# Attention in a two-layer hybrid backbone: the multiplication of the probabilities moves from VectorE to GpSimd

## The reference

```python
def softmax_with_sink(s, sink):                       # group A: 8 heads of 64, 2 KV heads
    m = jnp.maximum(jnp.max(s, axis=-1, keepdims=True), sink)
    e = jnp.exp(s - m)
    return e / (jnp.sum(e, axis=-1, keepdims=True) + jnp.exp(sink - m))

def mla_core(qn, qr, kn, kr, v):                      # group C: 4 heads, 96 wide
    s = (jnp.einsum('bqhd,bkhd->bhqk', qn, kn)
         + jnp.einsum('bqhd,bkd->bhqk', qr, kr)).astype(jnp.float32) * MLA_SCALE
    p = jax.nn.softmax(s, axis=-1).astype(v.dtype)
    o = jnp.einsum('bhqk,bkhd->bqhd', p, v)
```

## Time and profile before

| what | value |
|---|---|
| median of 3 runs | 1774.49 us (1768.44 to 1776.2) |
| the profiled execution, first to last instruction | 1772.8 us |
| TensorE busy | 1656.5 us, 93% |
| VectorE busy | 448.1 us, 25% |
| ScalarE busy | 309.7 us, 17% |
| GpSimd busy | 43.0 us, 2% |

### The profile page before, as it was taken

The page is one execution under the profiler, slowest core; times in us unless marked ns, Lnnn a source line. Parts: engine busy times, 40 slices in busy tenths (PEclk is TensorE's granted clock), DMA queues, the critical chain, the costliest instruction groups (busy, mean ns, idle before and its releaser), DMA issues.

```text
span 1772.8 us, 21037 instructions
## 1 busy us (share of the span) xinstructions
PE 1656.5 (93%) x7998; PEld 937.7 (53%) x7999; DVE 448.1 (25%) x1098; ACT 309.7 (17%) x721; POOL 43.0 (2%) x49
## 2 busy tenths in 40 slices
PE   3999879999999999999998999899989989999988
PEld 1454445444444444445665765685536555865464
DVE  1367794210000000003588330100201101001011
ACT  3135453210000000002345221000101010000110
POOL 1001000100000000000010100000000000000000
PEclk9999999999999999999999989999999999999999
DMA  9530610252141122115304269987799999977997
GB/s 379 223 143 0 246 41 25 89 223 91 71 166 71 71 73 93 71 71 231 125 11 180 73 255 422 390 291 278 292 420 421 422 422 422 377 269 290 422 421 324
DMA packets 56605, 394.76 MB, mean 223 GB/s; under 512 B 6480, under 2 KB 7888, under 8 KB 8912
## 3 DMA queue, kind: packets, MB, share of 16 engines
q1 hardware_dynamic: 56384, 393.63, 56.1%
q10 hardware_dynamic: 144, 0.01, 0.0%
HBM read 392.57 MB, written 1.05 MB: 222 GB/s over the span
## 4 chain that ended last, share of the span: by engine, by line
PE 79%; DMA 10%; DVE 7%; issue 2%; ACT 1%; SPq 1%; DVEq 0%; ACTq 0%
PE ps L688 17%; DMA ring<-in_stream 10%; PE ps L764 10%; PE ps L470 9%; PE ps L773 9%; PE ps L708 9%; PE ps L668 5%; PE ps L812 4%; PE ps L809 3%; PE ps L416 2%; PE ps L867 1%; PE ps L592 1%; PE ps L745 1%; PE ps L796 1%; DVE arena L1358 1%
## 5 line engine op out<-in xcount | busy, mean ns | idle before, releaser
L688 PE MATMUL ps<-hT,ring 128*128 128x512 f32 x704 | 302.7, 592 | 0.0
L764 PE MATMUL ps<-ring,arena 128*64 128x256 f32 x1056 | 243.2, 384 | 20.9 <-DMA ring<-in_stream 14.3
L767 PE MATMUL ps<-ring,arena 128*64 128x256 f32 x1056 | 243.7, 384 | 0.0
L688 PEld LDWEIGHTS ps<-hT,ring 128*128 128x128 f32 x704 | 133.5, 190 | 167.3 <-issue 166.4
L764 PEld LDWEIGHTS ps<-ring,arena 128*64 128x64 f32 x1056 | 139.9, 137 | 92.7 <-issue 33.6
L470 PE MATMUL ps<-hT,ring 128*128 128x512 f32 (+2 forms) x480 | 172.5, 515 | 2.4 <-ACT hT L921 2.2
L773 PE MATMUL ps<-ring,arena 128*128 128x256 f32 x704 | 155.6, 379 | 0.0
L708 PE MATMUL ps<-arena,ring 128*128 128x512 f32 x352 | 151.2, 592 | 0.0
L773 PEld LDWEIGHTS ps<-ring,arena 128*128 128x128 f32 x704 | 132.2, 190 | 17.1
L767 PEld LDWEIGHTS ps<-ring,arena 128*64 128x64 f32 x1056 | 140.0, 137 | 0.0
L470 PEld LDWEIGHTS ps<-hT,ring 128*128 128x128 f32 (+1 forms) x480 | 87.9, 185 | 81.7 <-issue 73.7
(11 more groups left out here) (188 smaller groups left out, 1345.7 us busy)
## 6 DMA issues: line engine op xcount, KB each, us to landing
ring<-in_stream SPq DMA_DIRECT2D x371, 1024.0 KB, 13.1
xT<-in_x SPq DMA_DIRECT2D x8, 256.0 KB, 4.2
cst<-in_consts SPq DMA_DIRECT2D x1, 1092.0 KB, 23.8
out_x<-xT SPq DMA_DIRECT2D x4, 256.0 KB, 2.6
par<-in_params SPq DMA_DIRECT2D x2, 75.0 KB, 2.3
cst<-in_consts SPq DMA_DIRECT2D x1, 128.5 KB, 2.2
moep<-in_moe SPq DMA_DIRECT2D x1, 36.0 KB, 25.5
ccol<-in_c ACTq DMA_DIRECT2D x1, 8.0 KB, 2.4
```

The source lines that it names most:

```text
L688: last = pe.matmul(ps[:, 2 * m + f % 2, :], ring[:, slot, m * 1024 + k * P:m * 1024 + (k + 1) * P], hT[:, k, :], start=(k == 0), stop=(k = ...
L764: a = pe.matmul(ps[0:64, b, 0:256], hTe[:, k, 0:64], ring[:, s1, k * 256:(k + 1) * 256], start=(k == 0), stop=(k == KD - 1))
L767: last = pe.matmul(ps[64:P, b, 0:256], hTe[:, k, 0:64], ring[:, s3, k * 256:(k + 1) * 256], start=(k == 0), stop=(k == KD - 1))
```

## The change

The two multiplications of `shares` go from VectorE's list to GpSimd's. VectorE ends with the reciprocal and raises a new semaphore, `share_ready`; GpSimd waits for it, multiplies both heads and raises `soft_done`. `rden` gets a second buffer. GpSimd's instruction is `tensor_scalar` with two multiplications (by `rden`, then by 1.0), where VectorE's had one.

```diff
-        rden = sb("rden", [P, 2])
+        rden = sb("rden", [P, 2, 2])
...
+        share_ready = sem("share_ready")
...
+            def shares(layer, a):
+
+                stream_ = attention_units(layer)[a][2]
+                n = att_at[layer, a]
+                b = n % 2
+                gps.wait_ge(share_ready, n)
+                for hh in range(2):
+                    v = probs[:, 2 * b + hh, 0:T - stream_ * NX]
+                    last = gps.tensor_scalar(v, v, rden[:, b, hh:hh + 1], 1.0, ALU.mult, ALU.mult)
+                last.then_inc(soft_done, 1)
+
...
                 last.then_inc(spread_done, 1)
+                for a in range(len(attention_units(layer))):
+                    shares(layer, a)
                 for norm in (1, 2) if layer == 0 else (3,):
                     add_squares(norm)
...
-                chained(dve.reciprocal(rden[:, :], total))
-                for hh in range(2):
-                    v = probs[:, 2 * b + hh, 0:w]
-                    last = dve.tensor_scalar(v, v, rden[:, hh:hh + 1], None, ALU.mult)
-                last.then_inc(soft_done, 1)
+                dve.reciprocal(rden[:, b, :], total).then_inc(share_ready, 1)
```

More of the change, by code:

```diff
@@ L1344, in shares @@
             def shares(layer, a):
-                kind, _, stream_, _ = attention_units(layer)[a]
+                kind = attention_units(layer)[a][0]
                 n = att_at[layer, a]
                 b = n % 2
-                w = T - stream_ * NX
                 dve.wait_ge(exp_done, n)
```

## The result

The changed kernel takes 1781.84 us (median of 19 runs), the kernel before, run beside it, 1776.2 (19 runs). The ratio is 1.0034, 95% interval 1.0023 to 1.0045: 4 to 8 us slower, about 6. Timed again with the last experiments it is 1.0038 (1.0025 to 1.0050). The forecast was +12.4 us. The direction was right, the size twice too large, and the profile shows that two terms of the sum were wrong in opposite directions. That 1781.84 us lies inside the stated range is in part luck: these two errors offset each other.

A forecast was written before the change was run, and what follows sets the result against it. Attention was taken as bound by hand-over delays between engines, no engine being full. Layer 0's +8.7 us and layer 1's +3.7 us summed to +12.4 us, on 1774.5 giving 1786.9 (predicted 1787 us), range 1771 to 1803 us.

The forecast's parts named there:

- The path: Attention: TensorE's transposes wait for the multiplication nearly everywhere, in layer 0 24.7 us, in 22 of 24 units.
- x: Attention, 512 columns: path lengthened by 2M - 0.84 us per multiplication step, 1.03 us at the middle price.
- The last two units: Layer 0's end, 256 columns: nothing runs beside them, so they pay y, together +1.1 us.
- y: Attention, 256 columns: path lengthened by 2m - 0.58 us per multiplication step, 0.54 us at the middle price.
- The four turns that TensorE fills: Layer 0, before units 14, 15, 18 and 19: TensorE runs through, so the change costs 0.
- The price M: One GpSimd multiplication of 512 columns: 0.936 us, the middle between its copy (0.609) and its addition (1.263).
- unit 5: Layer 0: VectorE's 1.28 us of deviations in its turn cover a longer multiplication up to about 1.1 us.
- VectorE's relief: Layer 0, six 256 wide units between those of group A: VectorE is the bound, 0.62 us won each, -3.7 us.
- VectorE against GpSimd: Attention: the two engines holding each other up, at most 0 to 0.94 us twice, taken as 0.
- the hold-up that the forecast named as a sign of being wrong: VectorE's small steps (L1338, L1340, L1353) lasting as long as GpSimd's multiplications would show the forecast wrong.
- The clock: Rival, attention: longer pauses lower TensorE's clock for a third of 36 turns, +10.6 us more, 1797 us; chance 0.06.
- One for one: After attention: what attention loses or wins moves all later work by the same amount.

The follow-up runs named there:

- e3: Changed kernel with one multiplication in GpSimd's instruction instead of two; ratio to the kernel before 1.0349.
- e9: The changed kernel unaltered, timed and profiled again; ratio to the kernel before 1.0038, the two attention stretches 6.2 us longer.
- e7: Changed kernel with TensorE's scores of unit a+3 ahead of the values of unit a-1 and VectorE's output copy a turn later; ratio to the kernel before 1.0026.
- e6: Kernel before with TensorE's scores of unit a+3 ahead of the values of unit a-1 and VectorE's output copy a turn later; ratio to the kernel before 0.9989.
- e2: Changed kernel with GpSimd multiplying each head twice, the second time by 1; ratio to the kernel before 1.0290.

## Why the prediction was half right

- **The path.** Right. The multiplication is on the path, and where a 512 wide unit's is, it costs what the formula says: x = 2 x 0.68 - 0.84 = 0.52 at the measured price, and eight turns of layer 0 got longer by 0.53 to 0.54 us. The last two units pay 0.37 (y = 0.36). The four turns that TensorE fills changed by 0.01.
- **The price M**, taken as 0.936 between copy and addition: mis-sized, it measured 0.68. This is the step that failed by most. At 0.68 the eleven units of layer 0 pay 5.7 us instead of 11.3, and the whole sum, worked again as in the forecast, is 5.7 - 0.6 (unit 5) - 3.7 + 0.7 = +2.1 us in layer 0 and -0.5 in layer 1 (0.1 for unit 0, 0.4 to unit 1, -1.6 to unit 8, -0.4 to unit 9, 1.0 at the end), 1.6 us instead of 12.4. "As far from one as from the other" was no argument, and "one stream in, one out" would have been none either: e3's instruction has the same streams and takes 1566 ns. What sets the price of a form, no run shows; it had to be measured.
- **VectorE's relief**, "the 0.62 are won: 6 x 0.62": wrong. In the nine turns between the transposes of units 1 and 4, 5 and 8, 9 and 12 the forecast's terms at the measured price give -3.3 us (+1.0 for two wide units, -0.6 for unit 5, -3.7); e9 against before shows -0.65. In layer 1 the relief from unit 1 to 8 is missing too: about -1.6 by the same terms, +0.4 measured. What relief there was showed mainly where VectorE has the convolution's work besides: from unit 5 to 6 (-0.74 us), from unit 10 to 12 (-0.60) and in layer 1 from unit 4 to 5 (-0.94). Elsewhere VectorE became idle for scores, or for transposes, before its relief reached the path; with the scores issued earlier 3.2 of the missing 4.6 us came back in these turns (e7). The forecast followed VectorE's list and GpSimd's chain, but not TensorE's, which delivers the scores to the former.
- Together: 1.6 at the right price, +4.6 for relief that did not come, is the 6.2 us of e9. The whole-time ratio, 6 us, agrees. The two errors have opposite signs, and that the kernel came out clearly slower is owed to the second: with the right price and the forecast's own relief it would have been a change of 0.1%.
- **VectorE against GpSimd**, taken as 0: about right. The two small sink steps lengthen from 161 to 199 and 191 ns on average in layer 0, group C's scaling of the maxima (L1356) from 170 to 251, and nothing waits for them. Five of these steps take 0.47 to 0.63 us, and each ends where GpSimd's pair of multiplications ends:
```profile
211.87 1.36 POOL L1146 TENSOR_SCALAR arena<-arena,rden 128x512 f32<-128x512 f32 x2 [2.66 <-DVE rden L1368]
...
212.60 0.63 DVE L1354 TENSOR_TENSOR sm<-nm,nsink 128x2 f32<-128x2 f32 x1
```
  So the hold-up that the forecast named as a sign of being wrong exists, now and then, and costs nothing here.
- **The clock**: in the changed kernel's two profiles the fall named among the rivals came on top once, for 1.6 us, and not in a third of the turns; e6 has the same fall without GpSimd. With longer pauses the rival does come true: e2 and e3 have a granted clock of 0.86 and 0.80 in layer 0.
- **One for one**: right up to the start of layer 1's attention, within 0.03 us. The end of the execution varies by more than the effect.

## What to carry to other kernels

Before counting an engine's relief, list for each of its steps what feeds it, and when: relief is worth only the time until the next input is late. A step given to an idle engine pays its hand-overs and its own slower rate in full if the next engine waits for it in every turn. And compare stretches cut at fixed instants when an effect is as small as the spread of executions: here they repeat to 0.1 us where the granted clock is the same, and where it is not (95.50 against 93.89 us for the same kernel) the clock of the stretch says so. Look at the clock of the timed executions as well, before a gain of some tenths of a per cent is credited to the kernel's code.

## What the runs showed of the hardware

- GpSimd's `tensor_scalar` on 128x512 float32 takes 700 ns with two operations, 621 with constants in place of the per-partition scalar, and 1566 with a single operation.
- GpSimd's and VectorE's multiplications side by side, VectorE's 0.06 us ahead: 486 ns for VectorE as alone, 983 for GpSimd instead of 700. The other way round, a VectorE step on 2 numbers per partition that came behind GpSimd's multiplications took 0.63 us instead of 0.16 and ended with them.
- TensorE's clock fell to its lower level behind a pause of 2.08 us in one profile and stayed at the upper behind the same pause in another.
- Executions with the same instructions differ by up to 14 us, and on the whole the shorter ones have the higher mean granted clock (the kernel before: 1781.16 us at 0.979, 1767.59 at 0.992).
